# Loading each expert matrix of a mixture-of-experts stage in two halves with a semaphore each

## What is computed

```python
DEPTH, SEQ, D_MODEL, N_EXPERTS, TOP_K, D_EXPERT = 2, 512, 1024, 16, 2, 512

for l in range(DEPTH):
    ...
    x = x + g1 * hybrid_mixer(h, w_in[l], ...)
    h = rms_norm(x, norm2[l]) * (1.0 + sc2) + sh2
    x = x + g2 * grouped_moe(h.reshape(B * S, D), w_router, router_bias,
                             w1[l], w3[l], w2[l]).reshape(B, S, D)
return rms_norm(x, norm_f)

def expert_block(args):          # of grouped_moe: the rows of one expert
    xb, e = args
    return (jax.nn.silu(xb @ w1[e]) * (xb @ w3[e])) @ w2[e]
```

## Time and profile before

| | us |
|---|---|
| median of 3 runs | 1641.25 (1639.93 to 1641.89) |
| profiled execution, its own time | 1639.41 |
| its span, first to last instruction | 1637.9 |
| PE busy | 1501.5 (92% of the span) |
| passes of the experts, layer 0, first L1711 to last L1722 | 563.67 to 814.57 |
| passes of the experts, layer 1 | 1355.93 to 1607.12 |

### The profile page before, as it was taken

The page is one execution under the profiler, slowest core; times in us unless marked ns, Lnnn a source line. Parts: engine busy times, 40 slices in busy tenths (PEclk is TensorE's granted clock), DMA queues, the critical chain, the costliest instruction groups (busy, mean ns, idle before and its releaser), DMA issues.

```text
span 1637.9 us, 19937 instructions
## 1 busy us (share of the span) xinstructions
PE 1501.5 (92%) x7140; PEld 732.3 (45%) x7141; DVE 471.8 (29%) x1136; ACT 436.2 (27%) x1029; POOL 67.8 (4%) x88
## 2 busy tenths in 40 slices
PE   4998999999999699999869999999999958999992
PEld 1574555544445433344336555554444533334440
DVE  0056554343332301111134463451111240111114
ACT  1426565300012211111132565551000221111111
POOL 1000000000000000000000000000000000000000
PEclk8999999999999699999979999999999978999996
DMA  9525143126150599999962432131404029999994
GB/s 353 215 80 190 45 130 129 52 65 205 52 193 26 212 418 423 419 424 422 364 237 103 145 117 104 32 124 39 140 14 154 26 86 399 420 419 423 420 393 173
DMA packets 87699, 343.45 MB, mean 210 GB/s; under 512 B 5396, under 2 KB 29556, under 8 KB 73256
## 3 DMA queue, kind: packets, MB, share of 16 engines
q1 hardware_dynamic: 61776, 305.68, 47.5%
q0 software_dynamic: 9168, 28.00, 4.6%
q10 hardware_dynamic: 16648, 8.40, 1.8%
HBM read 327.34 MB, written 17.86 MB: 211 GB/s over the span
## 4 chain that ended last, share of the span: by engine, by line
PE 87%; DMA 4%; DVE 3%; ACT 2%; issue 2%; DVEq 1%; SPq 0%; POOLq 0%; ACTq 0%
PE bank L1527 20%; PE bank L1711 18%; PE bank L1482 10%; PE bank L1722 9%; PE bank L1631 7%; PE bank L1542 4%; PE bank L1552 4%; PE bank L1562 4%; PE bank L1514 4%; PE bank L1458 2%; PE bank L1437 2%; DMA ring<-in_w_ada 2%; PE bank L1677 1%; DMA ring<-in_w 1%; PE bank L1617 1%
## 5 line engine op out<-in xcount | busy, mean ns | idle before, releaser
L1711 PE MATMUL bank<-ring,reg_b 128*32 128x512 f32 (+2 forms) x1376 | 285.0, 610 | 3.3 <-ACT reg_b L976 3.3
L1527 PE MATMUL bank<-hT,ring 128*128 128x512 f32 x512 | 222.7, 592 | 0.0
L1482 PE MATMUL bank<-ring,hT 128*128 128x512 f32 (+3 forms) x512 | 161.7, 477 | 1.5 <-ACT hT L837 1.5
L1711 PEld LDWEIGHTS bank<-ring,reg_b 128*32 128x32 f32 (+2 forms) x1376 | 94.6, 129 | 142.3 <-issue 140.3
L1527 PEld LDWEIGHTS bank<-hT,ring 128*128 128x128 f32 x512 | 97.0, 190 | 120.5 <-issue 120.5
L1482 PEld LDWEIGHTS bank<-ring,hT 128*128 128x128 f32 x512 | 98.7, 194 | 60.0 <-issue 31.0
L1527 PE MATMUL bank<-reg_a,ring 128*128 128x512 f32 x256 | 112.7, 593 | 0.8 <-DVE reg_a L1164 0.8
L1722 PE MATMUL bank<-ring,reg_b 128*32 128x512 f32 (+2 forms) x544 | 113.2, 594 | 0.0
L1631 PE MATMUL bank<-ring,reg_b 128*128 128x512 f32 x256 | 112.2, 593 | 0.0
L976 ACT ACTIVATE reg_b<-bank,cur 128x128 f32<-128x128 f32 x176 | 63.7, 468 | 178.7 <-PE bank L1677 178.7
L1159 DVE TENSOR_REDUCE nmax<-bank 128x1 f32<-128x512 f32 x128 | 84.2, 686 | 65.5 <-PE bank L1542 65.5
(11 more groups left out here) (224 smaller groups left out, 1479.5 us busy)
## 6 DMA issues: line engine op xcount, KB each, us to landing
ring<-in_w SPq DMA_DIRECT2D x74, 2048.0 KB, 23.7
ring<-in_w_ada SPq DMA_DIRECT2D x20, 2048.0 KB, 8.4
reg_a<-in_w SPq DMA_DIRECT2D x12, 2048.0 KB, 22.0
ring<-in_w_in SPq DMA_DIRECT2D x10, 2048.0 KB, 12.7
hT<-in_w SPq DMA_DIRECT2D x10, 2048.0 KB
vb<-in_w_ada ACTq DMA_DIRECT2D x16, 512.0 KB, 4.0
ring<-in_w_o SPq DMA_DIRECT2D x4, 2048.0 KB, 8.8
ring<-in_w_proj_a SPq DMA_DIRECT2D x8, 512.0 KB, 9.9
```

The lines of the kernel that those rows point to most:

```text
L1482: ins = pe.matmul(bank[2 + k % 4][:, 0:n], hT[:, c, t * P:(t + 1) * P], w[:, c, :], start=c == 0, stop=c == NC - 1)
L1527: ins = pe.matmul(gate_bank(j, q)[:, :], w[:, c, (j % 4) * P:(j % 4 + 1) * P], src[:, c + (4 if q == 3 else 0), :], start=c == 0, stop=c = ...
L1711: ins = pe.matmul(bank[bk][at:at + n, :], xsT[:, p % 2, c, at:at + n], slot(MOE_SLOT[j, m], NC, F)[:, c, :], start=c == 0, stop=c == NC - 1)
```

## The change

Each of the three helpers issues two DMAs of 1 MB in place of one of 2 MB. Of w1 and w3 the first half holds, in every partition, the four rows of chunks 0 to 3, a piece of 8 KB, and the second those of chunks 4 to 7. Of w2 the first half holds output columns 0 to 511 and the second columns 512 to 1023, so that a piece is 2 KB and a half has four of them per partition. The first half increments the slot's old semaphore; the second a new one (eight new ones). `loaded` stands where it was and now speaks of the first half only; the new `loaded_whole` waits for the second half ahead of chunk 4 of an up product, and ahead of half h = 1 of a down product.

```diff
+        w_rdy2 = [sem(f"slot{k}_second_half_loaded") for k in range(R + 2)]
...
                 def load_w1(j, e):
                     s = MOE_SLOT[j, 0]
-                    sp.dma_start(slot(s, NC, F), w1_v[l * E + e]).then_inc(w_rdy[s], 16)
+                    sp.dma_start(slot(s, NC, F)[:, 0:4], w1_v[l * E + e][:, 0:4]).then_inc(w_rdy[s], 16)
+                    sp.dma_start(slot(s, NC, F)[:, 4:8], w1_v[l * E + e][:, 4:8]).then_inc(w_rdy2[s], 16)
...
                 def load_w2(j, e):
                     s = MOE_SLOT[j, 2]
-                    sp.dma_start(slot(s, 4, D), w2_v[l * E + e]).then_inc(w_rdy[s], 16)
+                    sp.dma_start(slot(s, 4, D)[:, :, 0:512], w2_v[l * E + e][:, :, 0:512]).then_inc(w_rdy[s], 16)
+                    sp.dma_start(slot(s, 4, D)[:, :, 512:D], w2_v[l * E + e][:, :, 512:D]).then_inc(w_rdy2[s], 16)
...
+                def loaded_whole(j, m):
+
+                    s = MOE_SLOT[j, m]
+                    loads = [load for load in MOE_LOADS if load[2] == s]
+                    pe.wait_ge(w_rdy2[s], l * (16 * len(loads)) + 16 * (loads.index((j, m, s)) + 1))
...
                     for h in range(2):
+                        if h:
+                            for j in places(p):
+                                loaded_whole(j, 2)
                         for c in range(4):
...
                         for c in range(NC):
                             if p == 0 and c == 4:
                                 pe.wait_ge(tr_e, g)
+                            if c == 4:
+                                for j in places(p):
+                                    loaded_whole(j, m)
                             ins = up_tiles(p, m, 4 + m, c)
```

More of the change, by code:

```diff
@@ L560, in load_w1 @@
                     s = MOE_SLOT[j, 0]
-                    sp.dma_start(slot(s, NC, F), w1_v[l * E + e]).then_inc(w_rdy[s], 16)
+                    sp.dma_start(slot(s, NC, F)[:, 0:4], w1_v[l * E + e][:, 0:4]).then_inc(w_rdy[s], 16)
+                    sp.dma_start(slot(s, NC, F)[:, 4:8], w1_v[l * E + e][:, 4:8]).then_inc(w_rdy2[s], 16)
                 def load_w3(j, e):
                     s = MOE_SLOT[j, 1]
-                    sp.dma_start(slot(s, NC, F), w3_v[l * E + e]).then_inc(w_rdy[s], 16)
+                    sp.dma_start(slot(s, NC, F)[:, 0:4], w3_v[l * E + e][:, 0:4]).then_inc(w_rdy[s], 16)
+                    sp.dma_start(slot(s, NC, F)[:, 4:8], w3_v[l * E + e][:, 4:8]).then_inc(w_rdy2[s], 16)
                 def load_w2(j, e):
                     s = MOE_SLOT[j, 2]
-                    sp.dma_start(slot(s, 4, D), w2_v[l * E + e]).then_inc(w_rdy[s], 16)
+                    sp.dma_start(slot(s, 4, D)[:, :, 0:512], w2_v[l * E + e][:, :, 0:512]).then_inc(w_rdy[s], 16)
+                    sp.dma_start(slot(s, 4, D)[:, :, 512:D], w2_v[l * E + e][:, :, 512:D]).then_inc(w_rdy2[s], 16)
                 wait(sp, ga_r, l * 8 + 8)
```

## The result

The changed kernel takes 1644.83 us (median of 12 runs, 1643.08 to 1648.61) beside 1639.24 for the kernel before on the same chip (1637.08 to 1641.89, 12 runs): a ratio of 1.0032 with a 95% interval of 1.0022 to 1.0042. It was run twice more among the experiments, on other chips: 1.0015 [1.0004, 1.0025] and 1.0031 [1.0020, 1.0041]. So it is slower by about 4 us, 0.15 to 0.3%. The forecast, 1641.3, was too low; the slower rival had said 1645.7. The forecast stood on the three runs of the kernel before that were known, 1641.25, and added 0.05 us to them; against the median of twelve, 1639.24, the change is 5.6 us, so the forecast of the change is further off than 1644.83 beside 1641.3 looks.

What follows compares the result with a forecast made beforehand. PE was taken to set the pace in the experts' passes, DMAs just ahead; -0.55 + 0 + 0 + 0.6 = +0.05 us gave a median of 1641.3 us (chance 0.74), 8-in-10 range 1639.6 to 1645.8.

Steps and rivals of the forecast that it cites:

- slower rival: Full DMA stages: loads lose more than the margin, PE waits ahead of the last w2 product; 1645.7 us, chance 0.19.
- What bounds the kernel: Experts' passes: PE sets the pace, DMAs run just ahead; the last load's slack is 3.8 and 3.6 us.
- New waits on PE: 0: Middle of 33 products per layer: already fulfilled waits cost PE nothing; 0 us taken, bound 2.6 us.
- SP's second issue: 0: SP's load queue: 45 further issues of 0.35 us per layer are covered by the backlog; 0 us.
- The wait that goes: 0.5: w3 product of pass 1: first half lands earlier, so waits of 0.51 and 0.04 us go; gain 0.55 us.
- Smaller pieces: Expert loads: 0.31 us more per w2, 0.03 per w1 or w3; a layer's last load lands 5.5 us later.
- The margin: Last w2 product of a layer: slack plus half a load, 6.5 us (layer 0) and 6.3 (layer 1), against 5.5 delay.
- Tail of layer 0: Behind layer 0's passes: delayed w_in loads, ending near 822, cross the last scatter; 0.6 us, between 0 and 1.4.
- fixed cost: Rival: each of 44 more DMAs per layer shows its 3.0 us fixed time; 1890 us in all, chance 0.01.
- faster case: Rival: small pieces let gathers through sooner at the passes' start, clock helping; 2.5 to 3 us gained, 1638.5, chance 0.06.
- deciding point: Full DMA stages: an average loss from 0.14 us per load makes PE wait ahead of the last w2 product.

Runs made afterwards that it cites:

- down_rows: w1 and w3 halved as in the change, w2 halved by rows (4 KB pieces), against the kernel before: 1639.52 us beside 1639.85, ratio 0.9995.
- w2_rows16: Kernel before with w2 laid out in 16 KB pieces, hidden rows transposed to match, whole loads: 1641.22 us beside 1640.63, ratio 1.0002.
- up_only: Only w1 and w3 halved (8 KB pieces), w2 whole, against the kernel before: 1640.33 us beside 1639.85, ratio 1.0006.
- waits_alone: Kernel before with whole loads, PE asking again for the slot's semaphore in the middle of each product: 1641.40 us beside 1638.88, ratio 1.0009.
- down_only: Only w2 halved by columns (2 KB pieces), w1 and w3 whole, against the kernel before: 1642.25 us beside 1639.85, ratio 1.0017.
- halves_8k: All 48 matrices halved, w2 in 16 KB rows halved by rows, every piece 8 KB, against the kernel before: 1641.21 us beside 1640.63, ratio 1.0005.
- z_behind_after: Changed kernel with layer 1's second and third w_in loads issued behind the reload of ys_d, against the kernel before: 1641.60 us beside 1638.88, ratio 1.0012.
- the three on the left of the table: Profiled executions: kernel before, the same with two w_in loads behind the ys_d reload, and w2_rows16; layer 0 tails 20.1, 20.2, 19.6 us.
- again_2: The changed kernel itself run once more, against the kernel before on the same chip: 1645.46 us beside 1640.63, ratio 1.0031.
- again: The changed kernel itself run once more for a second profile, against the kernel before: 1642.47 us beside 1639.85, ratio 1.0015.
- up_partitions: Kernel before with w1 and w3 each in two DMAs of 64 partitions, 16 KB pieces, w2 whole: 1998.48 us beside 1640.63, ratio 1.2186.

## Why the prediction was wrong where it was

**What bounds the kernel** held. PE was busy for 100.00 us of 100 in the passes, and the experiments that moved the last landing by less than the slack left the time alone (down_rows, w2_rows16, up_only).

**New waits on PE: 0** held for PE: 0.43 us per step, in waits_alone and in the change. (What the prediction calls a chunk of 0.43 us is half of one; its 3.4 us for half a product are right.) The step overlooked that instructions are moved by the same DMAs. 66 waits, some with a register instruction, went with one further 16 KB packet in each last scatter, and scatters that are 0.8 to 1.6 us longer in the profile. No term of the sum had it; how much of it reaches the median isn't shown.

**SP's second issue: 0** held. SP stood at one issue for up to 19.9 us in layer 0 and 20.1 in layer 1, more than twice the 8.70 of the earlier trace rows, while the DMAs stayed full (share 1.02 and 1.01 in the two stretches of 10 us from 771), and down_rows shows that the second DMA of a w2 costs nothing. One effect was missed: a w_in load waits in that line too. The stop below stands at the first half of load 46; behind it load 47 was issued at 793.9 in place of 784.9, and the first w_in load at 799.1 in place of 785.5.

```profile
771.32 19.89 SPq L572 DMA_DIRECT2D hT<-in_w  x1
```

**The wait that goes: 0.5.** It went in all three executions of the changed kernel. But it is not a fixed 0.5: in executions with whole w1 and w3 the same place of layer 1 cost PE 0.3, 0.8, 1.5 and 1.8 us, and down_only 3.0; halves_8k kept 1.5 in spite of its halves. Load 8 landed 30.5, 30.9, 31.7, 31.1 and 32.3 us behind the issue of load 4 in these, and what moves either is not shown. A term of 0.5 read from one execution was one draw.

**Smaller pieces** is the first term that was mis-sized. The sum had 15 x 0.31 + 29 x 0.03 = 5.5 us; measured were 6.2 to 8.4 in the six layers of the changed kernel's three executions, 7.1 on average. The 2 KB term was right (0.23 to 0.32); the 8 KB one was 0.07 to 0.09 instead of 0.03. The fault was to read it from two rates of 428 and 432 GB/s, each good to 1%, where a difference of 2% was wanted. The trace has a better ruler, the median duration of a packet from 600 to 700 us: 612 ns for 16 KB, 313 for 8, 161 for 4, 86 for 2. Twice 313 is 2.3% above 612, or 0.11 us of a load of 4.90; twice 86 is 6.8% above 161, or 0.35 us of 5.11. By these the delay is 15 x 0.35 + 29 x 0.11 = 8.4 us, which is the price of the slower rival and the upper end of what was measured, as 5.5 is below its lower end. The fault lies in the small term alone.

**The margin** of 6.3 to 6.5 us was about right, and so it did not hold against 6.2 to 8.4: the product started 1.2 us late in layer 0 and 1.1 in layer 1, or 0.2 to 1.4 in the other two executions. What was left out is the clock: it was at the lower level behind the wait in two of the six last products of the changed kernel, at 1.7 us each. Over all runs it was so behind four of the seven idle stretches of 1.96 to 2.31 us there, and behind none of the shorter ones (0.87 to 1.63 us).

**Tail of layer 0** is the second term that was mis-sized: 0.6 us with a bound of 1.4, and 4.2 to 4.4 in the profiled executions. The crossing that was named did take place, and the third w_in load landed even later than foreseen, at 825.8 in place of 822. For the scatter itself the bound was wrong, because it took the 16 engines as one resource that two transfers share. The scatter's last packets came 8.4 to 8.8 us after its start in the changed kernel, 4.1 before, while all that moved in that time, 1.96 MB, is 4.8 us of DMA work at 410 GB/s. The DMAs' share (the last but one column) was 1.06 or more up to 819 and then fell while the scatter was still open, so much of the engines' time went unused:

```profile
822.00:823.00 1.00, 0.00 (x0) 0.00 (x0) 0.11 (x1) 0.00 (x0) 0.00 (x0) 0.50 0.41 143
824.00:825.00 1.00, 0.00 (x0) 0.00 (x0) 0.00 (x0) 0.00 (x0) 0.00 (x0) 0.50 0.19 75
```

z_behind_after prices the crossing at 3.3 us of the scatter, but only 1.4 of them came back in the tail, as much as the bound allowed. waits_alone, with w_in and all loads as before, has a tail of 21.7 us, 1.7 above the three on the left of the table. The remaining 1.2 us of the 4.3 are open, and so is how much of all this is in the medians, where tails of 23.0 and 23.5 us (down_rows, halves_8k) went with no loss.

**The rivals.** The slower one gave 1645.7 from 1.9 + 2.1 + 1.4 us. The time was near that, by another mix, so the nearness is luck: PE's waits 1.2 + 1.1, the clock 0 to 1.7, the tails 4.3 + 1.2. Its deciding point (0.14 us per load) was right: the least delay, 6.2 / 44 = 0.14, left PE 0.2 us late, and the largest, 8.4 / 44 = 0.19, 1.1 us. The fixed cost did not appear, nor did the faster case: the gather at the start of layer 1's passes takes 5.9 us of PE's time in place of 6.3.

**What is shown and what is open.** That the loss comes from the 2 KB pieces of w2 is shown: with as many DMAs and waits but pieces of 4 KB (down_rows) or 8 KB (halves_8k) it is gone. How the about 4 us divide is not: the waits for load 47 and the clock behind them stand in all three executions with 2.2 to 4.0 us together, less the 0.3 us or more that the wait in pass 1 gives back, and the tails are priced only by profiled executions that lie off the medians. Why the first comparison and that of again_2 differ from that of again is open too.

## What to carry to other kernels

A semaphore per half helps only where an engine waits for a load; here PE waited 0.3 to 1.8 us in one place of one layer, and a finer load paid for it in every packet. If a load must be cut, cut it so that the contiguous piece stays long (4 KB and 8 KB cost nothing that the time showed, 2 KB did) and all 128 partitions take part, and look at what stands behind the full queue: here the next layer's weights came 9 us later and crossed the last scatter. Compare piece sizes by the duration of their packets and by the landing of the last load, not by GB/s of short stretches. And take a stage's loss for a loss only when the medians show it: the profiled executions of several kernels here had tails 3 us longer without one.

## What the hardware showed that was not expected

**A DMA into 64 partitions runs at half the rate.** The DMA row and GB/s of up_partitions in 40 slices of 600 to 700 us:

```profile
DMA  9999999999799999999989999999999999999999
GB/s 216 224 206 244 220 229 197 223 210 216 159 367 442 244 197 242 203 223 210 210 175 352 415 413 411 434 211 213 229 203 216 210 210 182 211 379 415 336 169 205
```

All engines are busy throughout, at 210 GB/s while w1 and w3 come in by 64 partitions, at 415 while a whole w2 does. A packet of 16 KB takes 1255 ns in place of 612. Two such DMAs stand one behind the other in the queue, and don't make up for each other. This is what turned a question about 0.1 us into 358 us, with PE waiting and its clock down:

```profile
600.00:650.00 50.00, 30.02 (x214) 9.06 (x216) 2.77 (x4) 4.09 (x10) 0.80 (x1) 0.72 1.01 234
```

The Trainium skill (page "DMA: Bandwidth & Descriptors", section "The descriptor swizzle") has partitions 0 to 63 behind the even half of the 16 ports and 64 to 127 behind the odd half. The numbers fit that: 16 engines busy, half the rate. No run here tried another choice of 64 partitions.

**Instruction packets in the way of data.** Told under waits_alone: 16 KB in one packet, 0.9 to 2.3 us each, and a scatter that is 0.8 to 1.6 us longer beside one more of them.

**SP stands longer at an issue the smaller the pieces are.** Told under w2_rows16: at most 0.75 us with pieces of 16 KB alone, 3.3 with 8 KB alone, 8.7 with 16 and 4 KB, 20.6 with 8 and 2 KB.

**Packets have a fixed share of 9 to 14 ns.** Median durations at a full queue, 600 to 700 us, between two sizes each: 2 x 313 - 612 = 14, 2 x 161 - 313 = 9, 2 x 86 - 161 = 11 ns.
